# A two-model fp32 transformer kernel: splits, norms and tail in other places, the FFN gates' rows fetched through memory

## The reference, cut to what matters

```python
for i in range(2):
    mod = (silu(c) @ mod_w[i] + mod_b[i])             # 9 vectors of 1024
    sh0, sc0, g0, sh1, sc1, g1, sh2, sc2, g2 = split(mod, 9)
    h = rms_norm(x, norm_g[i, 0]) * (1 + sc0) + sh0
    x = x + 0.5 * g0 * swiglu(h, ffn_w_gu[i, 0], ffn_w_down[i, 0])
    h = rms_norm(x, norm_g[i, 1]) * (1 + sc1) + sh1
    x = x + g1 * (pool_mixer(h) if i == 0 else diff_attention(h))
    h = rms_norm(x, norm_g[i, 2]) * (1 + sc2) + sh2
    x = x + 0.5 * g2 * swiglu(h, ffn_w_gu[i, 1], ffn_w_down[i, 1])
x = rms_norm(x, final_g)
# second model: x + mix(rms_norm(x)), x + swiglu(rms_norm(x)), rms_norm(x) * final_g_2
```

## Time and profile before

| what | value |
|---|---|
| median of 3 runs | 1372.03 us (1371.13 to 1372.56) |
| the profiled execution | 1370.02 us, its span 1368.4 us |
| PE busy | 1327.4 us, 97% of the span |
| DVE busy | 947.3 us, 69% |
| ACT busy | 643.3 us, 47% |
| POOL busy | 154.9 us, 11% |
| moved by DMA | 304.8 MB, mean 223 GB/s |
| granted PE clock | 0.995 of full |

### The profile page before, as it was taken

How to read it: one execution, slowest core, us unless ns; L and a number is a source line. 1 busy time by engine, 2 the same in 40 slices (tenths; PEclk the granted TensorE clock), 3 DMA queues, 4 the chain that set the end, 5 groups by cost and what they waited for, 6 DMA issues and landing times.

```text
span 1368.4 us, 17814 instructions
## 1 busy us (share of the span) xinstructions
PE 1327.4 (97%) x6271; PEld 1080.2 (79%) x6271; DVE 947.3 (69%) x1125; ACT 643.3 (47%) x847; POOL 154.9 (11%) x227
## 2 busy tenths in 40 slices
PE   5999999999999999999999999999999999999997
PEld 3678888888888888888788778888887778888885
DVE  4788888779887788887677565465786557554442
ACT  3444334553333643335566643334665654643341
POOL 3110001200010100000232200010126000000000
PEclk9999999999999999999999999999999999999999
DMA  9999887499886699875543395564445435465540
GB/s 322 336 354 328 304 303 270 137 344 310 304 311 229 222 306 311 304 246 178 181 158 124 102 328 180 188 190 172 147 159 195 154 123 162 142 228 190 192 147 31
DMA packets 186070, 304.82 MB, mean 223 GB/s; under 512 B 8524, under 2 KB 134884, under 8 KB 185752
## 3 DMA queue, kind: packets, MB, share of 16 engines
q1 hardware_dynamic: 165432, 224.63, 48.8%
q0 software_dynamic: 20576, 79.37, 16.5%
HBM read 302.91 MB, written 1.05 MB: 222 GB/s over the span
## 4 chain that ended last, share of the span: by engine, by line
PE 86%; DVE 5%; DMA 3%; ACT 3%; issue 2%; POOL 1%; SPq 0%; POOLq 0%; DVEq 0%; ACTq 0%
PE ps L517 26%; PE ps L519 26%; PE ps L518 26%; DVE arena L1935 1%; PE ps L599 1%; DMA raw<-in_ffn_w_down 1%; DMA arena<-in_mod_w 1%; DVE wlo L1894 1%; DMA raw<-in_ffn_w_gu 1%; PE ps L626 1%; ACT whi L1292 1%; PE ps L635 1%; PE ps L672 1%; PE ps L948 1%; PE ps L970 0%
## 5 line engine op out<-in xcount | busy, mean ns | idle before, releaser
L1894 DVE TENSOR_TENSOR wlo<-raw,whi 128x2048 fp32r<-128x2048 f32 x212 | 481.5, 2295 | 89.6 <-ACT whi L1292 87.4
L517 PE MATMUL ps<-whi,nthi 128*128 128x512 f32 (+1 forms) x1264 | 506.7, 401 | 3.9 <-DVE ntlo L2218 1.7
L519 PE MATMUL ps<-whi,ntlo 128*128 128x512 f32 (+1 forms) x1264 | 493.7, 391 | 0.0
L518 PE MATMUL ps<-wlo,nthi 128*128 128x512 f32 (+1 forms) x1264 | 492.8, 390 | 0.0
L1292 ACT ACTIVATE whi<-raw 128x2048 fp32r<-128x2048 f32 x212 | 397.5, 1910 | 86.3 <-DMA raw<-in_ffn_w_gu 35.1
L517 PEld LDWEIGHTS ps<-whi,nthi 128*128 128x128 f32 x1264 | 238.7, 189 | 53.3 <-issue 5.8
L519 PEld LDWEIGHTS ps<-whi,ntlo 128*128 128x128 f32 x1264 | 238.5, 189 | 51.5
L518 PEld LDWEIGHTS ps<-wlo,nthi 128*128 128x128 f32 x1264 | 239.1, 189 | 45.3
L1935 DVE SCALAR_TENSOR_TENSOR arena<-arena,cact 128x512 f32<-128x512 f32 x238 | 178.8, 751 | 10.0 <-DMA arena<-in_mod_w 2.4
L517 PE MATMUL ps<-whi,hthi 128*128 128x512 f32 x440 | 172.9, 393 | 3.7 <-DVE htlo L1985 3.3
L519 PE MATMUL ps<-whi,htlo 128*128 128x512 f32 x440 | 171.6, 390 | 0.0
(11 more groups left out here) (276 smaller groups left out, 873.6 us busy)
## 6 DMA issues: line engine op xcount, KB each, us to landing
raw<-in_ffn_w_gu SPq DMA_DIRECT2D x176, 512.0 KB, 5.4
arena<-in_mod_w POOLq DMA_DIRECT2D x72, 1024.0 KB, 7.1
raw<-in_ffn_w_down SPq DMA_DIRECT2D x88, 512.0 KB, 5.7
raw<-in_w_in SPq DMA_DIRECT2D x44, 512.0 KB, 4.6
raw<-in_w_gate_up SPq DMA_DIRECT2D x44, 512.0 KB, 4.9
raw<-in_diff_w_qkv SPq DMA_DIRECT2D x24, 512.0 KB, 4.6
raw<-in_w_down SPq DMA_DIRECT2D x22, 512.0 KB, 5.8
raw<-in_diff_w_o SPq DMA_DIRECT2D x8, 512.0 KB, 4.0
```

The costliest lines, as they stand in the source:

```text
L517: pe.matmul(o, hi, wh, start=start, stop=False)
L518: pe.matmul(o, hi, wl, start=False, stop=False)
L519: return pe.matmul(o, lo, wh, start=False, stop=stop)
L1894: v.tensor_tensor(wlo[:, s * PIECE:(s + 1) * PIECE], raw[:, r * PIECE:(r + 1) * PIECE], hi, ALU.subtract).then_inc(w_lo, 1)
```

## The change

- The gates of ffn 0 to 3: PE turns the 8 columns at once into 8 rows of bank M, in front of the last column step, ACT copies them (times 0.5) to the tile `grow`, POOL sends them to memory (`gate_rows`, 4 KB), waits, and fetches them broadcast to 128 partitions into `gate` (512 KB). DVE's first `joined` waits for that fetch. POOL does this in `pass_gate`, behind the FFN's chunk loads and ahead of all that follows on its queue; in ffn 0 ahead of the load of MOD_LAST.
- The next to last down block of t = 0 is cut in two halves, with the turn of the inner tile (`turn_one`) between them, in all five FFNs.
- DVE's `one_lo` stands ahead of `keep_turned` of MOD_NINTH.
- Splits: one of DVE's and one of ACT's move from the join after the attention to the attention's end; one of DVE's in the join after ffn 2 moves ahead of `joined(1)`; one of ACT's in the head of ffn 3 moves behind `x_hi(1)`.
- `hold`: in the joins after ffn 2 and after the attention, DVE waits for rstd of t = 1 before its last split; in the final join, for rboth of t = 1.
- In the join after the attention ACT takes the first gated half ahead of `scaled_rows(1)`.
- In ffn 3, POOL loads MOD_TURN (2 MB) only when 8 pieces of that FFN are used.
- The end, for t = 1, goes by halves of 512 columns: sums, squares, the product with the row, the scaling (one half on ACT, one on DVE) and the output.

```diff
 @sync
-            for t in range(TB):
-                sp.wait_ge(y_ready, t + 1)
-                sp.dma_start(out[0, t * P:(t + 1) * P, :], xnt[:, t, :]).then_inc(out_done, 16)
+            sp.wait_ge(y_ready, 1)
+            sp.dma_start(out[0, 0:P, :], xnt[:, 0, :]).then_inc(out_done, 16)
+            sp.wait_ge(y_half, 1)
+            sp.dma_start(out[0, P:2 * P, BLK:D], xnt[:, 1, BLK:D]).then_inc(out_done, 16)
+            sp.wait_ge(y_ready, 2)
+            sp.dma_start(out[0, P:2 * P, 0:BLK], xnt[:, 1, 0:BLK]).then_inc(out_done, 16)
...
 @tensor, ffn
+            def turn_gate(cols_):
+                o = bank(M)
+                pe.transpose(o[0:KT, 0:P], cols_, ident[:, :]).then_inc(filled[M], 1)
...
                 turn_inner()
+                if gated is not None:
+                    turn_gate(gated)
...
-                down_block(d9, 1, 0, False, False)
+                down_block(d9, 1, 0, False, False, halves=(0,))
                 if MOD_NINTH[f]:
                     turn_chunk()
                 turn_one(0, A)
-                if gated is not None:
-                    gate_rows(gated, (B, M))
+                down_block(d9, 1, 0, False, False, halves=(1,))
...
-                down_block(d10, 0, 1, False, True).then_inc(w_used, 1)
+                if f == 4:
+                    down_block(d10, 0, 1, False, True, halves=(0,)).then_inc(last_half, 1)
+                    down_block(d10, 0, 1, False, True, halves=(1,)).then_inc(w_used, 1)
...
 @scalar, join
                 squares(1)
                 split(splits[3])
+                if gated:
+                    gated_half(0, full(A))
                 scaled_rows(1)
 @scalar, ffn_head
-                gated_half(0, full(A))
-                split(1)
+                if f != 3:
+                    gated_half(0, full(A))
+                    split(1)
                 one_hi(0, 0)
                 second_half(1, j, g_cols, shift)
                 x_hi(1, j)
+                if f == 3:
+                    split(1)
                 gated_half(1, full(B))
 @scalar, ffn
                 inner_hi(1)
+                if gated:
+                    n.next("gate")
+                    o = full(M)
+                    nc.scalar.activation(grow, o[0:KT, 0:P], ACT.Copy, scale=0.5).then_inc(drained[M], 1)
...
-                if gated:
-                    gate_rows(0.5, (B, M))
 @scalar, diff_attention, its end
                 gate_row(1, T, 1.0)
+                split(1)
 @scalar, main
-            j = join(*norm, (1, 0, 1, 1), silu_at=0)
+            j = join(*norm, (0, 0, 1, 1), silu_at=0, gated=True)
...
-            squares(1)
+            q = n.next("squares").at
+            for h in range(2):
+                act.wait_ge(x_ready, q + h + 1)
+                nc.scalar.activation(ps[:, 2 + h, :], x[:, 1, h * BLK:(h + 1) * BLK], ACT.Square,
+                                     accum_out=(ss, ssg)[h][:, 1:2]).then_inc(sq_done, 1)
+            act.wait_ge(z_row, 1)
+            act.wait_ge(rstd_done, 2 * TB + n.seen("norms") + 2)
+            nc.scalar.activation(xnt[:, 1, 0:BLK], xnt[:, 1, 0:BLK], ACT.Copy, scale=rstd[:, 1:2]).then_inc(y_ready, 1)
 @vector, ffn
+                one_lo(0, 0)
                 if c:
                     keep_turned(chunk_at(*MOD_NINTH[f]))
-                one_lo(0, 0)
 @vector, joined
+                    if t == 0 and gated in range(4):
+                        dve.wait_ge(gate_landed, 16 * (gated + 1))
 @vector, join
                 joined(1, last, gated)
+                r = n.next("rstd").at
+                if hold:
+                    dve.wait_ge(rstd_done, r + 1)
                 split(splits[2])
 @vector, final_join
                 gained(1)
+                dve.wait_ge(rboth_done, 2)
                 split(1)
 @vector, diff_attention, its end
-                split(1)
+                split(2)
 @vector, main
-            j, norm = join(**normed(1, 1), splits=(2, 0, 2), last=START["qkv"] - 1, tail=True)
+            j, norm = join(**normed(1, 1), splits=(2, 1, 1), last=START["qkv"] - 1, gated=2, tail=True, hold=True)
...
-            j, norm = join(**normed(1, 2), splits=(0, 0, 2), last=START["ffn3"] - 1, gated=(M, T))
+            j, norm = join(**normed(1, 2), splits=(0, 0, 1), last=START["ffn3"] - 1, gated=(M, T), hold=True)
...
+            for h in range(2):
+                if h == 0:
+                    dve.wait_ge(last_half, 1)
+                else:
+                    dve.wait_ge(w_used, START["end"] + 1)
+                c = slice(h * BLK, (h + 1) * BLK)
+                v.tensor_tensor(x[:, 1, c], x[:, 1, c], ps[:, 2 + h, :], ALU.add).then_inc(x_ready, 1)
+            for h in range(2):
+                dve.wait_ge(x_ready, done + h + 1)
+                c = slice(h * BLK, (h + 1) * BLK)
+                v.tensor_tensor(xnt[:, 1, c], x[:, 1, c], row[:, c], ALU.mult).then_inc(z_row, 1)
+            dve.wait_ge(z_row, 2)
+            dve.wait_ge(rstd_done, n.next("rstd").at + 1)
+            v.tensor_scalar(xnt[:, 1, BLK:D], xnt[:, 1, BLK:D], rstd[:, 1:2], None, ALU.mult).then_inc(y_half, 1)
 @gpsimd
+            def pass_gate(f):
+                turned = len(MOD_STEP[f]) + bool(MOD_HEAD[f]) + bool(MOD_TURN[f]) + (2 * TURNS if MOD_LOOP[f] else 0)
+                pool.wait_ge(drained[M], n.seen(M) + 2 * (f == 0) + turned + 1)
+                pool.dma_start(gate_rows[f].rearrange("(j p) -> j p", p=P), grow).then_inc(gate_sent, 16)
+                pool.wait_ge(gate_sent, 16 * (f + 1))
+                if f:
+                    pool.wait_ge(gate_used, 2 * GATE_JOIN[f])
+                pool.dma_start(gate[:, :], broadcast(gate_rows[f], D)).then_inc(gate_landed, 16)
 @gpsimd, load_chunks
                 if MOD_TURN[f]:
+                    pool.wait_ge(w_used, START[f"ffn{f}"] + 8)
                     load_chunk(*MOD_TURN[f])
...
+                pass_gate(f)
 @gpsimd, main, ffn 0
             pool.dma_start(band.rearrange("p g t s -> p (g t s)"), d["band"]).then_inc(band_landed, 16)
             pool.dma_start(mixed.rearrange("p k s -> p (k s)"), broadcast(d["bsum"], KT * S)).then_inc(shift_landed, 16)
+            pass_gate(0)
             load_chunk(*MOD_LAST[0], behind=1)
```

More of the change, by code:

```diff
@@ L1346, in step @@
                 inner_hi(par)
-            def gate_rows(scale, banks=(M, T)):
-                g = n.next("gate")
-                if g.first:
-                    act.wait_ge(gate_used, 2 * g.at)
-                for h, b in enumerate(banks):
-                    gate_row(h, b, scale)
             def gate_row(h, b, scale):
@@ L1404, in scaled_rows, with join @@
                     nc.scalar.activation(xnt[:, t, c], x[:, t, c], ACT.Copy, scale=r[:, t:t + 1]).then_inc(xs_ready, 1)
-            def join(g_cols, shift, splits, tail=None, silu_at=None):
+            def join(g_cols, shift, splits, tail=None, silu_at=None, gated=False):
                 j = n.next("join").at
@@ L2146, in ffn @@
                     keep_turned(chunk_at(*MOD_LOOP[f]) + 4 * (2 * TURNS - 1))
+                if gated:
+                    pass_by(M)
                 split(1)
@@ L2235, in pool_join, with join @@
                 return j, (scol[:, :], shift)
-            def join(g_cols, shift, splits, last, gated=(M, B), scale=None, tail=False):
+            def join(g_cols, shift, splits, last, gated=None, scale=None, tail=False, hold=False):
                 j = n.next("join").at
@@ L2265, in final_join @@
                 v.engine_nop().then_inc(g_ready, 1)
-                joined(0, last)
+                joined(0, last, 3)
                 gained(0)
@@ L2330, in pool @@
             def pool():
-                joined(0, START["pool"] - 1)
+                joined(0, START["pool"] - 1, 0)
                 split(1)
@@ L2341, in pool @@
                 add_chunk(halves=(1,), of=c)
-                joined(1, START["pool"] - 1)
+                joined(1, START["pool"] - 1, 0)
                 keep_chunk(chunk_at(*MOD_POOL))
```

58 lines of the change are left out of this document (33 added, 25 removed).

## The result

The changed kernel took 1364.48 us (median of 9 runs, 1362.46 to 1369.27), the kernel before, on the same chip, 1371.45 (9 runs, 1369.48 to 1372.73). The ratio is 0.9949, 95% interval 0.9937 to 0.9961: 7.0 us faster (5.3 to 8.6). The forecast took 8.7 off the median of three runs then at hand, 1372.0, which gave 1363.3.

A forecast was written before the change was run, and what follows sets the result against it. TensorE, busy 1327 of 1368 us, was taken to bound the kernel, so only its short waits could pay. Terms -4.4 + 2.5 - 2.3 - 4.6 + 1.8 - 1.7 = -8.7 on 1372.0 gave 1363.3 us, range 1358.5 to 1368.8.

The forecast's parts named there:

- FFN tails: Ffn 1 to 4: the half down block covers the turn's way back, without eight gate transposes; -4.4 us together.
- The gate's way: Gate through memory, ffn 1 to 3: write and fetch land before DVE's joined(0) needs them; cost 0.
- Ffn 0: Ffn 0 and pool stage: last chunk issued behind the gate's pass, so adds and sum_chunk start 2.5 late; +2.5 us.
- Join after ffn 2: Holding DVE's second split until rstd gives back 1.9 and 0.8, one split ahead of joined(1) costs 0.4; -2.3 us.
- Attention and ffn 3's head: Join after the attention and ffn 3's head: PE idles of 0.74, 1.37, 2.16 and small ones go; -4.6 us.
- third idle: PE's 2.16 us at 803.15 in ffn 3's head: gone through earlier SyncE loads and 2 MB of MOD_TURN delayed.
- Rival C: Ffn 3's head stays starved, the third idle coming from gate-up loads that crawl anyway; 2.7 less gain, 1366.0; chance 0.15.
- Rival D: Slower than before: the gate's round trip makes DVE wait in joined(0) of ffn 0 to 3; up to 1381.8; chance 0.05.
- Final join: Join after ffn 3: DVE's split held until rboth, PE starts 2.4 late, 0.6 of it comes back; +1.8 us.
- The end: After the last product: working by halves gives -1.55, the smaller last output -0.5, DVE slowing POOL +0.3; -1.7 us.
- The mix: The mix, behind the final join: no change predicted, 0.
- The sum: Whole kernel: the terms add up to -8.7 us, put on the median of 1372.0.

The follow-up runs named there:

- whole_d9: The changed kernel with the next to last down block of the first rows whole again ahead of the turn, gates still through memory: 1369.92 us, 0.9991.
- no_holds: The changed kernel without the two holds on rstd (joins after ffn 2 and after the attention), the final join's hold kept: 1365.59 us, 0.9952.
- turn_early: The changed kernel without GpSimd's wait for eight used pieces ahead of ffn 3's MOD_TURN load: 1367.9 us, 0.9976.
- halves_only: The kernel before with only the next to last down block split around the turn, the eight gate transposes still on TensorE: 1368.76 us, 0.998.
- both_undone: The changed kernel with ffn 0's last chunk's first half issued ahead of the gate's write and fetch, and no hold in the final join: 1360.82 us, 0.9925.
- final_free: The changed kernel without the hold on rboth ahead of DVE's split in the final join: 1361.68 us, 0.9931.
- slow_gate: both_undone with ffn 0's gate wait and fetch behind the second chunk half (1355.85 us), plus the gate written three times in ffn 1 to 3: 1364.3 us, 0.9949.
- chunk_first: The changed kernel with ffn 0's last chunk's first half issued ahead of the gate's write and fetch, the second half behind them: 1364.37 us, 0.9949.

## Why the prediction was right, and where it was not

**FFN tails** (-4.4): right. -1.20, -1.29 and -1.27 in ffn 1, 2 and 4; whole_d9 brings back 1.02 of idle in each, which is the covering that the step described. In ffn 3, which the table doesn't set apart, whole_d9 takes 1.25 longer. That transposes and half block only pay together was in the working and is now shown.

**The gate's way** (0): right in the sum, wrong in both parts: the write landed in 1.6 us in ffn 1 to 3 (I took 4.2), the fetch in 5.3 to 7.0 (I took 4.3). Together 7.6 in ffn 1, from the write's issue to the fetch's landing, against my 8.6. The write of the Trainium skill's page (DMA: Bandwidth & Descriptors, "Anatomy of one DMA"), 2.0 us, is closer than my row was; its 3.2 for the fetch is farther off. Behind a 1 MB half the write was seen only after 5.8, which neither had.

**Ffn 0** (+2.5): the step "the adds start 2.5 late, sum_chunk at 230.9" was right to 0.5 us (231.35). What failed is "the shift" as its only price. With PE's own tail shorter, the idle became 4.26, and the clock behind it fell: 3.1 more. The term had no price for the clock, and the bound of +4.5 didn't hold +6.07.

**Join after ffn 2** (-2.3): -2.48. The split of it was off: I gave the hold all of it (1.9 and 0.8), no_holds gives it 0.8, the rest, by what is left over, is the split that no longer runs beside rstd.

**Attention and ffn 3's head** (-4.6): about -4.9 (the stretch's -6.10 less a tail of 1.2). Of the third idle I named two causes; turn_early bears out one, the chunk's 2 MB, and halves_only, where the idle went with both causes in place, shows that they aren't all of it. Rival C (it stays) fell. **Rival D** fell for the changed kernel, and its mechanism was seen once, for 1.0 us, in both_undone.

**Final join** (+1.8): the mechanism was right and the size off. The step "PE starts 2.4 late" measured 2.42. "0.6 of that comes back" was wrong: final_free's turn follows its products at once, as in the kernel before, so there was nothing to come back. And the clock was missing again, 0 to 2.4.

**The end** (-1.7): -1.37 in the trace. Up to the last row of y it is 4.71 before and 3.50 after, -1.21 against the -1.25 of the working (1.55 less 0.3). What was mis-sized is "the last out is half as large: -0.5". From y to the span's end the trace gains only 0.16: 256 KB landed in 2.34 instead of 2.66, and its issue stood behind that of the other half. DVE's product runs until 1359.25 and POOL's operation, begun at 1358.98, takes 0.40 and ends behind it; alone such operations took 0.19 to 0.28. By the Trainium skill (SBUF — State Buffer, "Who interferes with whom") the end was worth 1.4, my estimate from its rule. The trace agrees with the mechanism, here and in the final join, where ss took 2.24 beside the split and 0.18 with DVE held. It doesn't agree with the size: some 0.2 was lost by it and not 0.6, so that 1.4 came out near the measured 1.37 is luck.

**The mix** (0): -1.74 in the profiled pair, from a stretch of seven slow products at 990 before that isn't there after. In the traces of the other kernels built on the changed one, none of which edits it, the mix took 189.95 to 191.72, so this differs between executions and is not shown to be the change's.

**The sum** (-8.7). The pair of traces has -4.6: the -8.7, with 3.57 and 3.05 more in the two places, 1.74 less in the mix and 0.8 less elsewhere. The medians have -7.0, and no trace says which of these costs the other executions had. The clock differs between them: the three runs at a granted 0.994 took 1362.5 to 1362.6, the five at 0.992 (the profiled one among them) 1364.5 to 1369.3. The time stayed inside the range because the range had room for a late chunk, not because the lower clock was foreseen. To that extent the hit is luck.

## What to carry to other kernels

An engine that issues loads must not stand in a wait with a load queued behind it that others need: send early, do the other issues, and wait only right ahead of the dependent one (5.0 us here by the medians, from one wait and the fetch behind it moved; in the traces 0.5 of it is PE's wait and 3.1 the clock behind it). An operation held back so that a small one of another engine runs freely is worth it only where PE waits for that small one: 0.8 us after ffn 2, nothing after the attention, a loss of 2.4 and more in the final join. And where an edit makes PE idle for a few us, count the clock behind the idle as part of its price: 1.5 to 3.1 us behind the nine idles of 2.46 to 4.83 ahead of sum_chunk.

## What the runs showed of the hardware that I had not expected

- Idles of PE between 2.46 and 4.83 us ahead of sum_chunk were followed in all nine traces that had them (slow_gate's 2.58 the ninth) by 7 to 12 products at a pitch of 0.43 instead of 0.23 us; after 1.93 none was. After the 3.09 of the final join it happened in five traces of six. With identity transposes in ffn 0's idle, or ahead of the pieces in the final join, it happened in neither place (one trace). At the first chunk's turn idles of 2.24 to 3.32 had such a stretch behind them in eight traces of thirteen. At the join after ffn 2 in the kernel before, 2.71 us idle had none. What decides between the cases the runs don't show.
- 4 KB written by GpSimd's queue landed in 1.6 us in ffn 1 to 3 of the changed kernel and in 1.6 to 4.2 in the same stages of the other traces. With 1 MB issued 2.6 us ahead on the same queue it took 4.1 to 6.3 (five traces; 5.5 in chunk_first).
- A VectorE split of 2.29 us stretched GpSimd's one-column operation from 0.18 to 2.24, to the end of the split (966.04 and 966.10 in final_free).
